# One decoder step: the output projection in two sums, a deeper attention pipeline, and the last down group by token chunks

## The reference

```python
z = rmsnorm(x, g_mix) @ w_in                       # eight parts: attention q, k, v, mLSTM inputs, gates
att = dilated window attention(q, k, v)            # 8 heads of 64; sample tokens also read a cache of 1024 rows
ml  = sigmoid(o) * mLSTM(...)                      # 8 heads of 64
cat = concat(rmsnorm(att, g_attn_out), rmsnorm(ml, g_mlstm_out))
h = x + cat @ w_out
h = h + cross_attention(rmsnorm(h, g_cross), memory)
hn = rmsnorm(h, g_ffn)
h = h + (silu(hn @ w_gate) * (hn @ w_up)) @ w_down
y = rmsnorm(h, g_final)
```

## Time and profile before

| | us |
|---|---|
| median of three runs | 2271.48 (2270.64 to 2275.33) |
| the profiled execution's own time | 2275.63 |
| its span, first to last instruction | 2273.7 |
| TensorE busy | 1994.4 (88%) |
| VectorE, ScalarE, GpSimd busy | 958.5, 421.2, 58.3 |
| granted TensorE clock, mean of the span | 0.939 |
| moved by the transfer engines | 188.97 MB, 83 GB/s on average |

### The profile page before, as it was taken

How to read it: one execution, slowest core, us unless ns; L and a number is a source line. 1 busy time by engine, 2 the same in 40 slices (tenths; PEclk the granted TensorE clock), 3 DMA queues, 4 the chain that set the end, 5 groups by cost and what they waited for, 6 DMA issues and landing times.

```text
span 2273.7 us, 29921 instructions
## 1 busy us (share of the span) xinstructions
PE 1994.4 (88%) x12998; PEld 1870.9 (82%) x12998; DVE 958.5 (42%) x1627; ACT 421.2 (19%) x751; POOL 58.3 (3%) x68
## 2 busy tenths in 40 slices
PE   6998888998477693988998689899999999999995
PEld 5996558998367452888897579899999999999994
DVE  7223662246565444448224123534333333333344
ACT  2004660001321034203104310300000000000013
POOL 3000000000121000000000000000000000000000
PEclk8999999999688696998999999999999999999997
DMA  4206602110054484124203421111111111111112
GB/s 157 86 28 224 225 2 56 38 45 11 14 204 149 156 347 182 47 65 126 88 12 127 153 70 41 34 46 37 46 47 46 35 58 38 44 42 50 36 33 79
DMA packets 164993, 188.97 MB, mean 83 GB/s; under 512 B 15815, under 2 KB 153575, under 8 KB 160042
## 3 DMA queue, kind: packets, MB, share of 16 engines
q1 hardware_dynamic: 163370, 154.19, 20.9%
q10 hardware_dynamic: 1536, 33.56, 3.8%
HBM read 170.95 MB, written 50.33 MB: 97 GB/s over the span
## 4 chain that ended last, share of the span: by engine, by line
PE 49%; DVE 2%; ACT 2%; issue 1%; DVEq 1%; DMA 0%; ACTq 0%
PE psum L254 45%; PE psum L1557 1%; ACT scratch L1578 1%; PE psum L1674 1%; DVEq L184 1%; DVE weights_lo L211 0%; DVE scratch L1615 0%; PE psum L1687 0%; PE psum L1546 0%; ACT wide L1735 0%; PE psum L1711 0%; PE psum L302 0%; DVE weights_hi L209 0%; PE psum L1506 0%; PE psum L1537 0%
## 5 line engine op out<-in xcount | busy, mean ns | idle before, releaser
L254 PE MATMUL psum<-x_lo,weights_hi 128*128 128x384 f32 (+1 forms) x2328 | 517.1, 330 | 0.0
L254 PE MATMUL psum<-x_hi,weights_hi 128*128 128x384 f32 (+1 forms) x2136 | 477.5, 332 | 32.6 <-DVE x_lo L292 19.1
L254 PE MATMUL psum<-x_hi,weights_lo 128*128 128x384 f32 (+1 forms) x2136 | 473.8, 330 | 0.0
L209 DVE CAST weights_hi<-weights_raw 128x1024 fp32r<-128x1024 f32 (+2 forms) x144 | 94.5, 656 | 843.6 <-PE psum L254 832.0
L254 PEld LDWEIGHTS psum<-x_lo,weights_hi 128*128 128x128 f32 x2328 | 401.4, 189 | 0.0
L254 PEld LDWEIGHTS psum<-x_hi,weights_hi 128*128 128x128 f32 x2136 | 367.9, 189 | 38.0 <-issue 27.1
L254 PEld LDWEIGHTS psum<-x_hi,weights_lo 128*128 128x128 f32 x2136 | 367.7, 189 | 0.0
L211 DVE TENSOR_TENSOR weights_lo<-weights_raw,weights_hi 128x1024 fp32r<-128x1024 f32 (+2 forms) x144 | 165.8, 1151 | 4.9
L254 PE MATMUL psum<-hidden_hi,weights_hi 128*128 128x384 f32 x528 | 117.2, 330 | 1.9 <-DVE hidden_lo L1826 1.9
L254 PE MATMUL psum<-hidden_hi,weights_lo 128*128 128x384 f32 x528 | 116.8, 329 | 0.0
L254 PE MATMUL psum<-hidden_lo,weights_hi 128*128 128x384 f32 x528 | 116.8, 329 | 0.0
(11 more groups left out here) (302 smaller groups left out, 2195.8 us busy)
## 6 DMA issues: line engine op xcount, KB each, us to landing
work<-in_cache_win_k_dram SPq DMA_DIRECT2D x8, 2048.0 KB, 10.3
work<-in_cache_win_v_dram ACTq DMA_DIRECT2D x8, 2048.0 KB, 11.7
weights_raw<-in_w_in_dram SPq DMA_DIRECT2D x28, 512.0 KB, 3.8
weights_raw<-in_w_gate_dram SPq DMA_DIRECT2D x22, 512.0 KB, 3.8
weights_raw<-in_w_up_dram SPq DMA_DIRECT2D x22, 512.0 KB, 3.7
weights_raw<-in_w_down_dram SPq DMA_DIRECT2D x24, 384.0 KB, 3.3
...
```

The source lines that it names most:

```text
L209: nc.vector.tensor_copy(whi[:, w, 0:nk, :], raw[:, w, 0:nk, :]).then_inc(w_high, 1)
L254: mm = nc.tensor.matmul(PS[:, 3 * s + c, 0:n], w[:, s, k], x[part][:, k, t0:t0 + n], start=(k == 0 and w is whi and part == 0), stop=(k == ...
```

## The change

- *Attention*: one more unit of distance. For unit u TensorE does the scores of u, the values of u-3 and the transposes of u-2. VectorE scales unit u-1 behind the logits of u. ScalarE does both exponentials of u-1 and then all copies of u-2. The first `order` rows show this for ScalarE.
- *Window*: three buffers for the keys and three for the values. Key block 2 is issued ahead of the state stores, value block 0 at the start of the stage; from there on the value loads are one block further ahead.
- *Two sums*: the products of a block of w_out are done for the mLSTM half (always into banks 0 to 2) and the attention half (always into banks 3 to 5) apart, on inputs that carry only the gain. VectorE multiplies each half by its own norm when it takes it out, and adds it to the residual. The squares of the two halves are summed by POOL, the attention's behind the attention stage, the mLSTM's during the window stage; the 64 sample columns of the attention by VectorE. The residual comes back in eight transfers. The barrier between window and projection is gone. The second `order` rows show a block on VectorE.
- *Last down group*: the three token chunks run one after the other, each over the eight blocks of w_down; the weights of blocks 2 to 7 are split into a space of their own (in the tile of x_hi). Inside, ScalarE squares the new residual and multiplies it by the gain, TensorE transposes it two steps later and sums the squares of a chunk's tokens, and VectorE scales by the norm in the token layout, from where SP stores. The barriers and the stage behind the group are gone. The third `order` rows show its start on TensorE.

The core of the diff:

```diff
-            for u in range(len(UNITS) + 2):
+            for u in range(len(UNITS) + 3):
                 if u < len(UNITS):
                     scores(u)
-                if u >= 2:
-                    values(u - 2)
-                if 1 <= u <= len(UNITS):
-                    turn(u - 1)
+                if u >= 3:
+                    values(u - 3)
+                if 2 <= u < len(UNITS) + 2:
+                    turn(u - 2)
...
-                if u >= 2:
-                    take(u - 2)
-                scale(u, 1)
+                if u:
+                    scale(u - 1, 0)
+                    scale(u - 1, 1)
+                if u >= 3:
+                    take(u - 3)
...
-            for u in range(len(UNITS) + 1):
-                for e in range(2):
-                    if u < len(UNITS):
-                        exponentials(u, e)
-                    if u:
-                        take(u - 1, e)
+            for u in range(len(UNITS) + 2):
+                if 1 <= u <= len(UNITS):
+                    exponentials(u - 1, 0)
+                    exponentials(u - 1, 1)
+                if u >= 2:
+                    take(u - 2, 0)
+                    take(u - 2, 1)
...
+        def att_squares_pool(pool):
+            chain = chains["pool"]
+            pool.wait_ge(o_taken, len(UNITS))
+            acc = att_sums[:, 0:SEQ]
+            chain(nc.gpsimd.tensor_tensor(acc, cat[:, 0, 0:SEQ], cat[:, 0, 0:SEQ], ALU.mult))
+            for k in range(1, NP):
+                chain(nc.gpsimd.tensor_tensor(att_square, cat[:, k, 0:SEQ], cat[:, k, 0:SEQ], ALU.mult))
+                last = nc.gpsimd.tensor_tensor(acc, acc, att_square, ALU.add)
+                if k + 1 < NP:
+                    chain(last)
+            last.then_inc(att_summed, 1)
...
         def load_k(sp, b):
-            if b >= 2:
-                sp.wait_ge(wk_turned, NP * 2 * (b - 1))
-            sp.dma_start(kc[:, b % 2, :].rearrange("p (t n) -> p t n", n=AW),
-                         A["cache_win_k"][b].rearrange("(p t) h d -> p t (h d)", p=P)).then_inc(kc_landed[b % 2], 16)
+            if b >= 3:
+                sp.wait_ge(wk_turned, NP * 2 * (b - 2))
+            sp.dma_start(kc[b % 3].rearrange("p (t n) -> p t n", n=AW),
+                         A["cache_win_k"][b].rearrange("(p t) h d -> p t (h d)", p=P)).then_inc(kc_landed[b % 3], 16)
...
             sp.wait_ge(phase_done, 4 * PH["sample"])
             load_k(sp, 1)
+            load_k(sp, 2)
...
         def win_load(sp):
-            for b in range(2, DB):
+            for b in range(3, DB):
                 load_k(sp, b)
...
+            load_v(act, 0)
             take_k(act, 0, 0)
             for b in range(DB):
                 if b + 1 < DB:
                     take_k(act, 0, b + 1)
                 if b == 0:
                     act.wait_ge(out_stored, 16 * mark["state"])
-                    load_v(act, 0)
                     load_v(act, 1)
+                    load_v(act, 2)
...
                     if b >= 3:
                         act.wait_ge(wo_ready, b - 2)
-                        load_v(act, b - 1)
-                        act.wait_ge(wo_ready, b - 1)
                         load_v(act, b)
+                        if b + 1 < DB:
+                            act.wait_ge(wo_ready, b - 1)
+                            load_v(act, b + 1)
...
+        def out_loads(sp):
+            w = [w_view(A["w_out"])]
+            sp.wait_ge(wo_ready, 6)
+            proj_load(sp, w, 2, NB["out"])
...
+            for j in (0, 1, 2, 4, 5, 6, 7, 3):
+                if j == 3:
+                    sp.wait_ge(wo_turned, DB // 2)
+                sp.dma_start(XT[:, j, :], XT_DRAM[:, j * N:(j + 1) * N]).then_inc(xt_back[j // 4], 16)
+            proj_load(sp, w, 8, NB["out"], start=2)
+        def out_tensor_halves(pe):
+            n0 = NB["out"]
+            pe.wait_ge(rnorm_ready, J["ml"][1] + 1)
...
+            for j in range(KB):
+                pe.wait_ge(w_split, n0 + j + 1)
+                if j:
+                    pe.wait_ge(ml_half_taken, j)
+                products(0, (xhi, xlo), NP, CHUNKS, (lambda k: None) if j else ml_first, (n0 + j) % 2, NP).then_inc(ml_half_ready, 1)
+                if j:
+                    pe.wait_ge(z_taken, n0 + j)
+                products(1, (xhi, xlo), NP, CHUNKS, (lambda k: None) if j else att_first, (n0 + j) % 2, 0).then_inc(z_ready, 1)
...
+        def out_vector_halves(dve):
+            chain, n0 = chains["dve"], NB["out"]
+            split_at(dve, n0)
+            for k in range(NP):
+                low(dve, sig_o, xhi[:, NP:], xlo[:, NP:], k, N, G_ML, J["ml"][2])
+            split_at(dve, n0 + 1)
+            for k in range(NP):
+                low(dve, cat, xhi, xlo, k, N, G_ATT, J["att"][2])
+            dve.wait_ge(rnorm_ready, J["ml"][1] + 1)
+            for j in range(KB):
+                split_at(dve, n0 + j + 2 if j + 2 < KB else NB["mk"] + j + 2 - KB) if j else None
+                dve.wait_ge(ml_half_ready, j + 1)
+                for c, (t0, w) in enumerate(CHUNKS):
+                    last = nc.vector.tensor_tensor(out_part[:, 0, t0:t0 + w], PS[:, c, 0:w], nr_ml[:, t0:t0 + w], ALU.mult)
+                last.then_inc(ml_half_taken, 1)
+                if j % 4 == 0:
+                    dve.wait_ge(xt_back[j // 4], 64)
+                dve.wait_ge(ml_half_taken, j + 1)
+                chain(nc.vector.tensor_tensor(XT[:, j], XT[:, j], out_part[:, 0], ALU.add))
+                if j == 0:
+                    split_at(dve, n0 + 2)
+                    dve.wait_ge(rnorm_ready, J["att"][1] + 1)
+                dve.wait_ge(z_ready, n0 + j + 1)
+                for c, (t0, w) in enumerate(CHUNKS):
+                    last = nc.vector.tensor_tensor(out_part[:, 1, t0:t0 + w], PS[:, 3 + c, 0:w], nr[:, t0:t0 + w], ALU.mult)
+                chain(last)
+                nc.vector.tensor_tensor(XT[:, j], XT[:, j], out_part[:, 1], ALU.add).then_inc(z_taken, 1)
+                if j:
+                    add_square(dve, nacc, j - 1, N, J["cross"][0])
...
+        def last_split(dve, j):
+            b = NB[f"down{LAST}"] + j
+            w = b % 2
+            dve.wait_ge(w_landed[w], 16 * (b // 2 + 1))
+            nc.vector.tensor_copy(d_hi[:, j - 2], raw[:, w, 0:LK, :]).then_inc(w_high, 1)
+            dve.wait_ge(w_high, b + 1)
+            nc.vector.tensor_tensor(d_lo[:, j - 2], raw[:, w, 0:LK, :], d_hi[:, j - 2].bitcast(F32), ALU.subtract).then_inc(w_split, 1)
...
+        def last_tensor(pe):
+            n0, z0 = NB[f"down{LAST}"], NB["ffn0"] + KB * LAST
+            def turn(i):
+                c, j = STEPS[i]
+                pe.wait_ge(f_gain, i + 1)
+                if i >= 2:
+                    pe.wait_ge(y_taken, i - 1)
+                for a, (t, n) in enumerate(TILES[c]):
+                    mm = nc.tensor.transpose(PS[0:n, 4 + i % 2, a * P:(a + 1) * P], f_gained[i % 2][:, a * P:a * P + n], IDENT[:, :])
                 mm.then_inc(y_turned, 1)
...
+            pe.wait_ge(gate_taken, LQ0 + LK)
+            pe.wait_ge(up_taken, LQ0 + LK)
+            for i, (c, j) in enumerate(STEPS):
+                t0, w = CHUNKS[c]
+                if c == 0:
+                    pe.wait_ge(w_split, n0 + j + 1)
+                if i >= 4:
+                    pe.wait_ge(z_taken, z0 + i - 3)
+                hi, lo = (whi[:, (n0 + j) % 2], wlo[:, (n0 + j) % 2]) if j < 2 else (d_hi[:, j - 2], d_lo[:, j - 2])
+                for k in range(LK):
+                    if i == 0:
+                        pe.wait_ge(h_low, LQ0 + k + 1)
+                    for a, (wk, x) in enumerate(((hi, ghi), (hi, glo), (lo, ghi))):
+                        mm = nc.tensor.matmul(PS[:, i % 4, 0:w], wk[:, k], x[:, k, t0:t0 + w], start=(k == 0 and a == 0),
+                                              stop=(k == LK - 1 and a == 2))
+                mm.then_inc(z_ready, 1)
+                if i >= 2:
+                    turn(i - 2)
+                if c and j == 3:
+                    token_sums(c - 1)
+            turn(len(STEPS) - 2)
+            turn(len(STEPS) - 1)
+            token_sums(2)
...
+            def scale(c, tiles):
+                dve.wait_ge(rnorm_ready, J["final"][1] + c + 1)
+                dve.wait_ge(y_taken, KB * (c + 1))
+                for a in tiles:
+                    n = TILES[c][a][1]
+                    y = y_tok[c % 2][0:n, a, :]
+                    nc.vector.tensor_scalar(y, y, f_norm[0:n, c, a:a + 1], None, ALU.mult).then_inc(y_scaled, 1)
+            for i, (c, j) in enumerate(STEPS):
+                t0, w = CHUNKS[c]
+                if c == 0 and j + 2 < KB:
+                    last_split(dve, j + 2)
+                dve.wait_ge(z_ready, n0 + i + 1)
+                x = XT[:, j, t0:t0 + w]
+                nc.vector.tensor_tensor(x, PS[:, i % 4, 0:w], x, ALU.add).then_inc(z_taken, 1)
+                if i:
+                    add_squares(i - 1)
+                if c and j == 5:
```

(25 more changed lines are left out.)

367 lines of the change are left out of this document (183 added, 184 removed).

## The result

The changed kernel took 2256.7 us (median of 4 runs, 2254.0 to 2258.2) against 2272.3 us for the kernel before in the same series: ratio 0.9927, 95% interval 0.9915 to 0.9939. It is 15.6 us faster, where 37 were forecast, and 2.7 us above the upper end of the range. Measured again beside other kernels, the ratio was 0.9930 (0.9908 to 0.9952). Its profiled execution took 2258.22 us (span 2256.1), 17.4 less than the one before.

The account below looks back on a forecast made before the run. TensorE, busy for 88% of the span, was taken as the bound, so only its waits could give. Terms 17 - 3 + 9.9 + 13 = 36.9 us gained led to 2234.5 us, range 2212 to 2254.

Parts of the forecast that it names:

- The projection and the gap ahead of it: Output projection: 32.8 us gained from the gap, 31.2 lost in six stalls with low clock, 4.2 at the end.
- The rival that the clock would hold: Projection: no fall of the clock in the six stalls, 10 us less, 2224 us; chance 0.15.
- the one that it would stay down: Projection: the clock stays at 1.2 GHz through blocks 2 to 7, slower, 2297 us; chance 0.05.
- The last group: Last down group to the end of the span: 71.5 us for 84.6, 13 us gained, bounds 5 and 17.
- The gate products: Behind the attention: GpSimd's squares lengthen the gate split, gap 4 us, then low clock; 3 us lost, bounds 0 and 5.
- The step "Attention": Attention: exponentials issued one unit earlier loosen the chain and TensorE is the bound; 17 us gained, bounds 0 and 22.
- The step "Window stage": Window stage: third buffers let loads go earlier; 12.5 us gained, bounds 0 and 17.
- the term of 8 us for the keys: Window stage: the 11.8 us key wait goes, 2 us each charged for blocks 1 and 2; 8 us gained.
- The 5 us for the last value loads: End of the window stage: a third buffer brings the load before the last a pair earlier; 5 us gained.
- That the transfers bound the stage, the rival: Window stage: more loads in flight end no earlier, 12.5 us missing, 2247 us; chance 0.10.
- the two rivals: Attention gains nothing, 17 us missing, 2251 us, chance 0.13; transfers bound the window stage, 12.5 missing, 2247 us, chance 0.10.

Follow-up runs that it names:

- the first experiment: Changed kernel with VectorE taking and adding the mLSTM half of a projection block before splitting the weights two blocks on: 2223.3 us, ratio 0.9760.
- its experiment: Changed kernel with GpSimd starting the squares of the attention output only after VectorE has split the gate weights: 2252.8 us, ratio 0.9904.
- the fastest kernel: Changed kernel plus projection take before split, stores on GpSimd, three banks, later squares, earlier norms, value load 0 behind key block 1's copies: 2202.5 us, ratio 0.9688.

## Why the prediction was wrong

- *The projection and the gap ahead of it: right.* The gap went as forecast (34.9). The stalls came at the places named, six, 3.54 us for 3.5, ended by the product with the mLSTM norm. Five of them cost 1.7 of clock, as forecast: a block behind a gap took 13.73 us (920.97 to the end of the block at 934.70) where one without takes 12.0 (the casts of the first experiment follow each other at that distance). Only behind the first was it 3.0: there the clock was at half for 6 us (902.44 to 908.4) and not for some 3.2; why, no run shows. The end of the projection waited 10.2, the number forecast. The rival that the clock would hold is refuted, and so is the one that it would stay down.
- *The last group: right in the sum, partly by luck*, 13.6 for 13.1. The last product ended 56.3 us behind the fourth hidden block for 58.2, and the tail behind it took 14.7 for 13.3 (its items add up to 13.5). The second chunk's norm so near the end, which I had not counted, cost 1.9 of that; two misses cancel.
- *The gate products: right in mechanism.* The gap is 3.82 for 4.0, the longer low part is shown by its experiment, and the rows give 3.1 us for the 3 forecast. That the longer gap is what brings the clock down is not shown.
- *The step "Attention": wrong in size.* I took it that TensorE is the bound once the chain is loosened, let the 8.3 us for the values go whole and three quarters of the 12.5 for the transposes. The values still wait 3.2 us and the transposes 9.0; the scores wait 4.6 where it was 2.0 (both in the lists of waits). That is 6.0 less in all, which is what the old order put back costs. I had read the wait for the transposes as the exponential between two copies. It is mostly the copies themselves, through two banks: a third bank takes it away. And the deeper chain empties one unit later, 1.6 us. The stretch without the gate gap gained 8.4 for 17, and 6.0 of that is the order.
- *The step "Window stage": wrong in size.* I counted what each transfer would win for its own reader, and charged 2 us for sharing. What failed is the term of 8 us for the keys. The loads put ahead of the state stores stretched the issue of eight stores from 9.12 to 19.20 us, and two things were queued behind the stores: key block 3 on SP, and a wait on ScalarE ahead of the copies of key block 2. TensorE got 4.18 and 6.94 us there for the 11.81 removed. Value load 0, which I had booked as part of the gain, cost 3.6 us alone. The 5 us for the last value loads did come: TensorE waited 6.3 us for them before (4.00 and 2.28) and 1.49 now. That the transfers bound the stage, the rival, doesn't hold: with the same loads the stage came down to 97.2 us in the fastest kernel.
- *The range.* The rivals were priced one by one. Half of the attention's gain and two thirds of the window stage's were missing together (8.6 and 8.5 us), and the upper end of the range left room for one of the two rivals, not for a part of both with 1.7 more in the projection.
